# Attention scores on VectorE in one instruction per score map, and the sample's exponentials at another place in ScalarE's queue, in a streaming encoder step

## The reference, cut to what matters

```python
def diff_attention(q, k, v, q_pos, k_pos, lam, rel_bias):
    s = jnp.einsum('bqhmd,bkhmd->bhmqk', q, k).astype(jnp.float32) * (HEAD_DIM ** -0.5)
    bias = jnp.moveaxis(rel_bias.astype(jnp.float32)[t5_bucket(k_pos[None, :] - q_pos[:, None])], -1, 0)
    visible = (k_pos[None, :] // CHUNK) <= (q_pos[:, None] // CHUNK)
    s = jnp.where(visible, s + bias[None, :, None], NEG_INF)
    pr = jax.nn.softmax(s, axis=-1)
    pr = pr[:, :, 0] - lam * pr[:, :, 1]
    return jnp.einsum('bhqk,bkhd->bqhd', pr, v.astype(jnp.float32))
```

## Time and profile before

| | us |
|---|---|
| runs | 1438.44, 1450.09, 1450.82 |
| median of the runs | 1450.09 |
| the profiled execution | 1445.04 |
| its span | 1443.1 |
| PE busy in the span | 1405.9 |
| DVE busy | 603.6 |
| ACT busy | 270.8 |

### The profile page before, as it was taken

One profiled execution on the slowest core, in us unless ns is written; L12 is line 12 of the kernel. 1 busy time (PEld: TensorE's weight loads), 2 busy tenths in 40 slices (PEclk: granted clock), 3 DMA queues, 4 the chain that ended last, 5 costly groups with the idle time before them and its releaser, 6 DMA issues.

```text
span 1443.1 us, 20551 instructions
## 1 busy us (share of the span) xinstructions
PE 1405.9 (97%) x7066; PEld 713.5 (49%) x7066; DVE 603.6 (42%) x1236; ACT 270.8 (19%) x661; POOL 116.3 (8%) x137
## 2 busy tenths in 40 slices
PE   8999999999999999999999999999999999999998
PEld 5787446554333333334456884565544333333344
DVE  6076775465310110105640677755653101101276
ACT  1211335212100110111121102453121001100111
POOL 3100000110000000003000000001100000000210
PEclk9999999899999999999999999999999999999999
DMA  9714103354699999957031132034546999999921
GB/s 301 273 60 137 44 1 121 146 195 146 235 375 400 424 426 427 384 221 279 34 134 59 59 109 72 1 119 149 195 146 205 354 426 420 428 426 428 346 103 48
DMA packets 81229, 319.49 MB, mean 221 GB/s; under 512 B 12716, under 2 KB 15076, under 8 KB 56588
## 3 DMA queue, kind: packets, MB, share of 16 engines
q1 hardware_dynamic: 67348, 273.25, 48.7%
q0 software_dynamic: 9280, 29.68, 5.6%
q10 hardware_dynamic: 4536, 15.71, 2.7%
HBM read 404.05 MB, written 29.67 MB: 301 GB/s over the span
## 4 chain that ended last, share of the span: by engine, by line
PE 88%; DMA 5%; DVE 3%; issue 2%; ACT 1%; DVEq 1%; POOL 0%; SPq 0%; ACTq 0%; POOLq 0%
PE psum L1394 22%; PE psum L970 12%; PE psum L1421 10%; PE psum L1038 8%; PE psum L1254 8%; PE psum L1493 7%; PE psum L940 4%; DMA region<-in_w_exp_up_dram 3%; PE psum L1373 2%; PE psum L904 2%; PE psum L878 2%; PE psum L1023 1%; PE psum L1311 1%; DMA ring<-in_w_ple_gate_dram 1%; PE psum L1060 1%
## 5 line engine op out<-in xcount | busy, mean ns | idle before, releaser
L1394 PE MATMUL psum<-ring,xT 128*64 128x512 f32 x800 | 354.0, 594 | 6.0 <-issue 3.5
L1395 PE MATMUL psum<-region,xT 128*64 128x512 f32 x800 | 354.2, 595 | 0.0
L1394 PEld LDWEIGHTS psum<-ring,xT 128*64 128x64 f32 x800 | 106.7, 137 | 220.7 <-issue 217.8
L1421 PE MATMUL psum<-ring,region 128*64 128x512 f32 x400 | 178.0, 597 | 4.7 <-issue 3.0
L1422 PE MATMUL psum<-region 128*64 128x512 f32 x400 | 178.1, 598 | 0.0
L970 PE MATMUL psum<-xT,ring 128*128 128x272 f32 x768 | 176.5, 393 | 0.0
L970 PEld LDWEIGHTS psum<-xT,ring 128*128 128x128 f32 x768 | 146.0, 190 | 29.8
L2307 DVE COPY region<-psum 128x512 f32<-128x512 f32 x23 | 15.9, 692 | 315.0 <-PE psum L1422 315.0
L1038 PE MATMUL psum<-ring,xT 128*128 128x512 f32 (+1 forms) x288 | 132.5, 603 | 0.6 <-DVE region L1962 0.6
L1493 PE MATMUL psum<-ring,xT 128*128 128x512 f32 x256 | 112.7, 595 | 0.8 <-ACT xT L1535 0.6
L783 POOL TENSOR_TENSOR rr<-rq,half 128x1 f32<-128x1 f32 (+4 forms) x41 | 56.8, 1386 | 698.3 <-DVE rq L1814 266.2
(11 more groups left out here) (295 smaller groups left out, 1481.0 us busy)
## 6 DMA issues: line engine op xcount, KB each, us to landing
region<-in_w_exp_gate_dram SPq DMA_DIRECT2D x50, 1024.0 KB
ring<-in_w_exp_gate_dram SPq DMA_DIRECT2D x50, 1024.0 KB
region<-in_w_exp_up_dram SPq DMA_DIRECT2D x50, 1024.0 KB
ring<-in_w_exp_up_dram SPq DMA_DIRECT2D x50, 1024.0 KB
ring<-in_w_exp_down_dram SPq DMA_DIRECT2D x50, 1024.0 KB
region<-in_w_exp_down_dram SPq DMA_DIRECT2D x50, 1024.0 KB
ring<-in_w_in_dram SPq DMA_DIRECT2D x24, 1024.0 KB, 7.6
expert_results<-region ACTq DMA_DIRECT2D x21, 512.0 KB, 7.8
```

The costliest lines, as they stand in the source:

```text
L1394: pe.matmul(bank[b][front, :], xeT[:, kc, front], ring[:, BLOCK_SLOT[u], kc % 4, :], start=kc == 0, stop=kc == KC - 1)
L1395: m = pe.matmul(bank[b][last, :], xeT[:, kc, last], back[:, UNIT_ROOM[u], kc % 4, :], start=kc == 0, stop=kc == KC - 1)
L1421: pe.matmul(bank[5 + half][front, :], hT[:, 2 * n + q, front], ring[:, BLOCK_SLOT[u], 2 * q + half, :], start=n + q == 0, stop=n + q == 2)
```

## The change

Four parts.

**One instruction for scale, bias and extreme value.** Per unit the pair of L2018 and L2021 (each over both maps) gives way to two `tensor_tensor_reduce`, one per map: out = (score + bias) * -1/8, and at the same time the minimum of the row of out, starting from 3e38, into `nmax`. Scores are so stored negated, and the minimum of the negated row is what the negated maximum was. The exponentials get `scale=-1.0`. `s_used` is gone; PE waits for `s_max` in its place. In the sample the four instructions of L2100 and L2101 and the maximum of L2103 become four such instructions, a drain and one `tensor_tensor` that takes the smaller of the two partial minima.

**Bias scaled beforehand.** As the bias is now added before the scale, `bias_p` and `bias_s` are multiplied by 8 once, behind L1871.

**No drain** stands between the scores and the extreme value in the prompt's units.

**ScalarE's order.** The wait for `ss_max` and the sample's two exponentials stand ahead of the loop that copies turns 5, 6 and 7.

```diff
-        s_used = sem("score_used")
@@ PE, attention step
                         if u >= 1:
-                            pe.wait_ge(s_used, n_att * l + u)
+                            pe.wait_ge(s_max, n_att * l + u)
@@ ScalarE, attention step
-                                              bias=nmax[:, u % 3, m2:m2 + 1], accum_out=psm[:, u % 3, m2:m2 + 1])
+                                              bias=nmax[:, u % 3, m2:m2 + 1], scale=-1.0, accum_out=psm[:, u % 3, m2:m2 + 1])
@@ ScalarE, after the attention
                 cache_in(2)
                 cache_in(3)
+                sc.wait_ge(ss_max, l + 1)
+                for m2 in range(2):
+                    m = sc.activation(sp[:, m2, :], sp[:, m2, :], ACT.Exp, bias=nmax[:, 0, m2:m2 + 1], scale=-1.0, accum_out=psm[:, 0, m2:m2 + 1])
+                m.then_inc(ss_exp, 1)
                 for n in range(TILES, len(TURNS)):
                     turned_in(n, *TURNS[n])
-                sc.wait_ge(ss_max, l + 1)
-                for m2 in range(2):
-                    m = sc.activation(sp[:, m2, :], sp[:, m2, :], ACT.Exp, bias=nmax[:, 0, m2:m2 + 1], accum_out=psm[:, 0, m2:m2 + 1])
-                m.then_inc(ss_exp, 1)
@@ VectorE, before the layers
             ve.memset(bias_p[0:CHUNK, :, 512 - CHUNK:512], NEG)
+            ve.drain()
+            ve.tensor_scalar(bias_p[:], bias_p[:], HD ** 0.5, None, ALU.mult)
+            ve.tensor_scalar(bias_s[:], bias_s[:], HD ** 0.5, None, ALU.mult)
@@ VectorE, attention step
-                        ve.scalar_tensor_tensor(pbuf[:, u % 3, :, 0:nk], psum[:, 0:2, 0:nk], HD ** -0.5,
-                                                bias_p[:, h, 512 - nk:512].unsqueeze(1).to_broadcast([P, 2, nk]), ALU.mult, ALU.add).then_inc(s_used, 1)
-                        ve.drain()
-                        ve.tensor_reduce(nmax[:, u % 3, :], pbuf[:, u % 3, :, 0:nk], X, ALU.max, negate=True).then_inc(s_max, 1)
+                        for m2 in range(2):
+                            m = ve.tensor_tensor_reduce(pbuf[:, u % 3, m2, 0:nk], bank[m2][:, 0:nk], bias_p[:, h, 512 - nk:512], -HD ** -0.5, BIG,
+                                                        ALU.add, ALU.min, nmax[:, u % 3, m2:m2 + 1])
+                        m.then_inc(s_max, 1)
@@ VectorE, the sample
-                    ve.scalar_tensor_tensor(sp[:, m2, 0:PAST], psum[:, 2 * m2:2 * m2 + 2, :].rearrange("p a b -> p (a b)"), HD ** -0.5, bias_s[:, 0:PAST], ALU.mult, ALU.add)
-                    ve.scalar_tensor_tensor(sp[:, m2, PAST:NKEY], bank[4 + 3 * m2][:, 0:DEC], HD ** -0.5, bias_s[:, PAST:NKEY], ALU.mult, ALU.add)
-                ve.drain()
-                ve.tensor_reduce(nmax[:, 0, :], sp, X, ALU.max, negate=True).then_inc(ss_max, 1)
+                    ve.tensor_tensor_reduce(sp[:, m2, 0:PAST], psum[:, 2 * m2:2 * m2 + 2, :].rearrange("p a b -> p (a b)"), bias_s[:, 0:PAST], -HD ** -0.5, BIG,
+                                            ALU.add, ALU.min, nmax[:, 1, m2:m2 + 1])
+                    ve.tensor_tensor_reduce(sp[:, m2, PAST:NKEY], bank[4 + 3 * m2][:, 0:DEC], bias_s[:, PAST:NKEY], -HD ** -0.5, BIG,
+                                            ALU.add, ALU.min, nmax[:, 2, m2:m2 + 1])
+                ve.drain()
+                ve.tensor_tensor(nmax[:, 0, :], nmax[:, 1, :], nmax[:, 2, :], ALU.min).then_inc(ss_max, 1)
```

More of the change, by code:

```diff
@@ L40 @@
 NEG = -1e30
+BIG = 3e38
 CHUNK = 64
```

## The result

The changed kernel takes 1458.39 us, the median of 16 runs (1452.12 to 1465.71); the kernel before took 1447.81 us beside it (16 runs, 1438.32 to 1453.38). The ratio is 1.0082, with an interval of 1.0063 to 1.0102: about 0.8% slower, 10.6 us. The forecast was 1462.5, in a range of 1449 to 1470. The profiled execution of the changed kernel took 1453.71 us, with a span of 1451.8; that of before took 1445.04, with a span of 1443.1, so the two traces are 8.7 us apart.

A forecast was written before the change was run, and what follows sets the result against it. PE, busy 97% of the span, was taken to bound the kernel. Stand +10.2, clock +3.0 and attention -0.6 gave +12.6 us on a base of 1450.1: 1462.7, stated as 1462.5, range 1449 to 1470.

The forecast's parts named there:

- A: Whole kernel: PE stands about 5 us a layer and the clock costs a little more; 1462.7 us, chance 0.58.
- Part 4, the stand: Sample's exponentials ahead of the retention copies: product(0, 0) waits, PE stands 5.1 us a layer, 10.2 in all (9.4 to 10.9).
- None of it is given back: Sample softmax: no later wait of PE takes up the stand's 5.1 us a layer; the earlier ss_done was not waited for.
- The table load: ScalarE, before the sample's exponentials: 1.28 us costed at nothing; if it waited for ss_max, 1.28 us a layer, +2.6.
- Part 1: Prompt's attention, one instruction per map: DVE 0.8 to 1.1 us shorter a step at 512 keys, worth -0.6 us in all.
- Parts 2 and 3: Bias times 8: about 2.2 us in DVE's idle time, costs nothing; sample's scores: ss_max at 271.82 in place of 273.61.
- rival C: New score instruction runs at half L2018's rate: the stand grows by 2.3 us a layer, 1467 us; chance 0.08.
- TensorE's clock behind the stand: First products after PE's stand: clock falls, 2.5 us at half clock, 1.5 us a layer, 3.0 in all (0 to 5.3 a layer).
- The base: Starting time of the kernel before: 1450.1 us, median of three runs, taken as a run with a clock fall in both layers.
- rival D: Clock falls ahead of the products do not come, each worth 5.3 us: not slower, 1449 to 1452 us; chance 0.18.
- B: Clock stays low behind the stand as long as in layer 0: 5.3 us a layer, +7.6, 1470 us; chance 0.12.
- E: Attention is bound by DVE: L2021's time comes off the span, -22.8 against +13.2 from part 4, 1440.5 us; chance 0.04.

## Why the prediction was right

The forecast was 1450.1 + 12.6 = 1462.7, a change of +12.6; measured was 1458.39, and +10.6 against the kernel before beside it. Its mechanism, A, is the one that the traces show, and the time stayed within 1% of before, to which the forecast gave 0.59. By its steps:

- **Part 4, the stand: right in kind, 10% too large.** Forecast 5.1 us a layer, measured 4.64. The order of events is the forecast's. DVE took 2.84 us from the first score instruction to `ss_max` (262.08 to 264.92) and not 3.19, since the accumulator's read, taken as 0.1 us for each instruction, costs nothing (80 ns, beside the next instruction), and the exponentials with the first copy took 2.95 us (264.96 to 267.91), forecast 3.08. "None of it is given back" held. The table load was free as forecast: it ran at 260.42, ahead of the wait.
- **Part 1: right.** -0.75 us for both layers' attention, forecast -0.6, which was also its outer bound. DVE's 25 us less work gave back the one wait that PE had.
- **Parts 2 and 3: right.** The scaling took 1.9 us under an idle time of over 11; rival C fell with 687 ns for 512 elements, where half of L2018's rate would have been 1.22 us. The half was the author's supposition; no run shows such a rate.
- **TensorE's clock behind the stand: the mis-sized term.** Forecast 1.5 us a layer, for 2.5 us at half clock; measured 2.90 and 2.37. The clock fell in the stand, as expected, but it came back only after 5.9 us of dense products in layer 0 and 4.8 in layer 1, not 2.5. The 2.5 us are read from the earlier trace rows: L1198's dense scores begin at 260.69, and the clock, 0.50 in 262:263 and 0.90 in 263:264, is back at about 263.2. What failed is to take the time from the first dense matmul to the return for the price of a return. PE had been busy all along since 250, at a clock of 0.50, so the rows showed when the fall ended, not how long a fall lasts. The bounds, 0 and 5.3 a layer, held.
- **The base: one fall too many.** With the terms as measured the sum is 9.28 + 5.27 - 0.75 = 13.8, and 1450.1 + 13.8 = 1463.9. The 5.5 us to 1458.39 are about the price of one fall in the retention stretch. The prediction took a run with two falls as the median run of both kernels. That the changed kernel's median run has one fewer is read from the groups of times, and no trace shows a run with falls in both retention stretches. The 16 runs of the changed kernel lie in groups at 1452 to 1454 (3 runs), 1457 to 1460 (10) and 1462 to 1466 (3), the 16 of before at 1438 to 1440 (4), 1444 to 1447 (4) and 1449 to 1454 (8). The median of the sixteen of before is 1447.81, already 2.3 under the base that three runs gave. By this reading rival D was half of the truth: not that the falls don't come, but that the median run has one fewer. It was listed as a rival; it should have been a term with a size of its own, as the runs shown of before, the profiled one among them, already stood at 1438.4, 1445.0 and 1450.
- **Rivals B and E fell.** B's price, 5.3 us for each layer's stand, was twice what came; E's attention did not get shorter by more than 0.4 us a layer.

Two misses, +2.3 on the clock behind the stand and -5.5 on the base, partly hid each other. With the clock's term right, the forecast would have been 1465.0 and 6.6 us off in place of 4.3; that much of its nearness is luck.

## What to carry to other kernels

Moving work to the front of an in-order queue charges everything behind it with that work's wait, and the price is paid by the first thing behind it that the bottleneck engine needs: here one of three copies decided, and moving the exponentials one copy further back took all of the 9.3 us away. If TensorE is 97% busy, look at its granted clock and at its small waits that lie close together before looking for work to save elsewhere: filling two waits of half a us a layer with idle matmuls was worth 0.5 to 0.6% here, where the new scores with 25 us less work on DVE gave 0.3%, and next to nothing once the waits were filled. And if a kernel's runs lie in groups, find what separates the groups and give it a term, before pricing a change against their median.

## What the runs showed of the hardware

- In a stand of 4.89 us PE's clock fell to 0.50 and stayed there for about 6.8 us in both layers, 5.9 and 4.8 of them dense matmuls; the first product took 9.96 and 9.44 us in place of 7.06. With four idle matmuls in the second half of the stand it stayed at 1.00 and took 7.07.
- The clock also fell, from 1.00 to 0.50, where PE had only short waits: four of 0.18 to 0.62 us within 7 us, in layer 0's retention stretch, in eight of nine profiled runs with no idle matmul in it. In layer 1's stretch, with waits between the same bounds, it fell in none of the nine. With two of the waits filled it fell in one profiled run of four. Which runs fall is not fixed: kernels without the fill have runs of both kinds.
- DVE's instruction that adds, scales and takes the row's minimum at once ran at 687 ns for 512 and 1222 ns for 1024 f32 elements, as long as the instruction that it replaces (1.22 us for 1024); its accumulator's read, 80 ns, ran beside the next instruction (both start at 211.97).
- Each idle f32 matmul stands in the trace as two instructions: one of 128x256 took 0.60 us in the attention and 0.70 in the retention stretch, a pair 1.13, four of 128x512 3.70.
